# Summing two weight parts of a seven-product block form on GpSimd instead of VectorE

## The reference, cut to what matters

```
proj = rmsnorm(x, ln_g) @ w_in
q, k, v, z_a, x_b, z_b, g_a, g_b = split(proj)
...
merged = sigmoid(g_a) * (o_a @ w_a) + sigmoid(g_b) * (o_b @ w_b)
x = x + merged @ w_o
```

## Time and profile before

| | before |
|---|---|
| median of 3 runs (lowest, highest) | 1893.27 us (1892.89, 1893.54) |
| span of the profiled execution | 1889.0 us |
| time around the span, median less span | 4.3 us |
| TensorE (PE) busy | 1872.9 us, 99% |
| VectorE busy | 1306.7 us, 69% |
| ScalarE busy | 827.0 us, 44% |
| GpSimd busy | 298.6 us, 16% |

### The profile page before, as it was taken

The page is one execution under the profiler, slowest core; times in us unless marked ns, Lnnn a source line. Parts: engine busy times, 40 slices in busy tenths (PEclk is TensorE's granted clock), DMA queues, the critical chain, the costliest instruction groups (busy, mean ns, idle before and its releaser), DMA issues.

```text
span 1889.0 us, 32627 instructions
## 1 busy us (share of the span) xinstructions
PE 1872.9 (99%) x13004; PEld 1755.0 (93%) x13004; DVE 1306.7 (69%) x2260; ACT 827.0 (44%) x1352; POOL 298.6 (16%) x417
## 2 busy tenths in 40 slices
PE   9999999999999999999999999999999999999998
PEld 8899898898899999999998988988988999999997
DVE  7775665665766877866797656657557678878575
ACT  5432322423436776543444324234124377766334
POOL 2220120120231210100132201202102422001010
PEclk9999999999999999999999999999999999999999
DMA  6444534553443333543655445534444534337253
GB/s 220 137 129 159 179 132 130 163 180 110 150 147 96 104 99 99 155 134 105 199 175 162 148 124 170 178 110 152 168 119 146 167 97 107 96 93 183 90 167 116
DMA packets 119958, 264.06 MB, mean 140 GB/s; under 512 B 12510, under 2 KB 52942, under 8 KB 119678
## 3 DMA queue, kind: packets, MB, share of 16 engines
q1 hardware_dynamic: 87950, 159.94, 27.3%
q0 software_dynamic: 31712, 102.04, 17.5%
q10 hardware_dynamic: 144, 0.00, 0.0%
HBM read 203.11 MB, written 49.12 MB: 134 GB/s over the span
## 4 chain that ended last, share of the span: by engine, by line
PE 87%; DVE 5%; ACT 3%; DMA 2%; DVEq 1%; issue 1%; ACTq 1%; SPq 0%
PE bank L2414 19%; PE bank L2416 19%; PE bank L2415 19%; PE bank L2508 4%; PE bank L2509 4%; PE bank L2510 4%; PE bank L2778 2%; PE bank L2781 2%; PE bank L2780 2%; DMA w_raw<-in_w_units 2%; PE sums L2526 2%; PE sums L2508 1%; PE sums L2510 1%; PE sums L2509 1%; PE sums L2641 1%
## 5 line engine op out<-in xcount | busy, mean ns | idle before, releaser
L2414 PE MATMUL bank<-xn_hi,w_hi 128*128 128x296 f32 (+1 forms) x2016 | 603.5, 299 | 1.1 <-DVEq L2324 0.5
L2416 PE MATMUL bank<-xn_lo,w_hi 128*128 128x296 f32 (+1 forms) x2016 | 598.9, 297 | 0.0
L2415 PE MATMUL bank<-xn_hi,w_lo 128*128 128x296 f32 (+1 forms) x2016 | 598.1, 297 | 0.0
L2414 PEld LDWEIGHTS bank<-xn_hi,w_hi 128*128 128x128 f32 x2016 | 379.0, 188 | 8.4 <-issue 6.0
L671 ACT ACTIVATE w_hi<-w_raw 128x1024 fp32r<-128x1024 f32 x219 | 230.2, 1055 | 349.0 <-DMA w_raw<-in_w_units 346.4
L2415 PEld LDWEIGHTS bank<-xn_hi,w_lo 128*128 128x128 f32 x2016 | 379.5, 188 | 0.9
L2416 PEld LDWEIGHTS bank<-xn_lo,w_hi 128*128 128x128 f32 x2016 | 378.6, 188 | 0.0
L681 DVE TENSOR_TENSOR w_lo<-w_raw,w_hi 128x1024 fp32r<-128x1024 f32 x219 | 268.4, 1229 | 59.1 <-ACT w_hi L671 52.5
L2414 PE MATMUL bank<-oa_hi,w_hi 128*128 128x296 f32 (+1 forms) x512 | 153.7, 300 | 0.0
L2415 PE MATMUL bank<-oa_hi,w_lo 128*128 128x296 f32 (+1 forms) x512 | 151.9, 297 | 0.0
L2416 PE MATMUL bank<-oa_lo,w_hi 128*128 128x296 f32 (+1 forms) x512 | 151.7, 296 | 0.0
(11 more groups left out here) (347 smaller groups left out, 3846.1 us busy)
## 6 DMA issues: line engine op xcount, KB each, us to landing
w_raw<-in_w_units SPq DMA_DIRECT2D x189, 512.0 KB, 3.7
w_raw<-in_w_units SPq DMA_DIRECT2D x151, 256.0 KB, 3.4
S<-in_state_ret POOLq DMA_DIRECT2D x64, 512.0 KB, 4.8
out_ret_s<-S POOLq DMA_DIRECT2D x64, 512.0 KB, 6.2
w_raw<-in_w_units POOLq DMA_DIRECT2D x20, 256.0 KB, 4.9
vst<-v_scr SPq DMA_DIRECT2D x8, 512.0 KB, 4.1
out_ret_p<-Sp POOLq DMA_DIRECT2D x8, 512.0 KB, 5.9
v_scr<-vtok_hi SPq DMA_DIRECT2D x16, 160.0 KB
```

Source lines behind the costliest of these rows:

```text
L2414: pe.matmul(ps, w_hi[:, slot, cols], x_hi, start=first, stop=False)
L2415: pe.matmul(ps, w_lo[:, slot, cols], x_hi, start=False, stop=False)
L2416: return pe.matmul(ps, w_hi[:, slot, cols], x_lo, start=False, stop=last)
```

## The change

For the four pairs of g_b (not for the output projection's pairs) the sums S2 and S4 are made by GpSimd, between the adding transfers. GpSimd's queue per pair becomes: adding transfer of S1; wait for S2's load and for the landing of S1's transfer; add; drain; adding transfer of S3; wait for S4's load; add; drain. VectorE loses its eight adds and drains per layer and gets two waits per pair: it must not overwrite S1 before S2's sum has read it, nor S2 before S4's sum has.

```diff
@@ -960,9 +960,21 @@
+                def add_raw(two, part, other):
+
+                    n, m = two * PRODUCTS + part, two * PRODUCTS + other
+                    wait_part(pool, l, n)
+                    if other == S1:
+                        pool.wait_ge(s1_in[two % 2], 16 * pairs_like(l, two))
+                    pool.tensor_tensor(part_of(w_raw, l, n), part_of(w_raw, l, n), part_of(w_raw, l, m), ADD)\
+                        .then_inc(part_sum, 1)
+                    pool.drain()
+
                 for two in range(TILE_PAIRS):
                     add_part(two, S1)
+                    add_raw(two, S2, S1)
                     add_part(two, S3)
+                    add_raw(two, S4, S2)
                 load_early(0)
@@ -2073,6 +2085,8 @@
                     n = two * PRODUCTS + part
                     dve.wait_ge(part_hi, PART_AT[l] + n + 1)
+                    if two < TILE_PAIRS and part in (S1, S2):
+                        dve.wait_ge(part_sum, (PAIR_AT[l] + two) * 2 + (1 if part == S1 else 2))
                     dve.tensor_tensor(part_of(w_lo, l, n), part_of(w_raw, l, n), part_of(w_hi, l, n).bitcast(f32),
                                       SUB).then_inc(part_lo, 1)
@@ -2114,10 +2128,8 @@
                 part_low(0, A11)
-                part_add(0, S2, S1)
                 part_low(0, S1)
                 right_low(2, mix2_lo[:, :, 0:wide], of_right(mix2), mix2_hi[:, :, 0:wide])
-                part_add(0, S4, S2)
                 part_low(0, S2)
@@ -2138,9 +2150,7 @@
                     if more:
-                        part_add(two + 1, S2, S1)
                         part_low(two + 1, S1)
-                        part_add(two + 1, S4, S2)
                         part_low(two + 1, S2)
```

## The result

The kernel after takes 1902.15 us (median of four runs, 1900.78 to 1902.82), the kernel before 1893.08 in the same session: 1.0044 times, with a 95% interval of 1.0029 to 1.0058. That is 9.1 us slower, beyond the 0.2% (3.8 us) that a measurement can tell from no change. The profiled span is 1900.9 us, 11.9 above that of before; of this, the block forms hold 8.8, and 2.5 are one wait in layer 0's output projection, told at the end of the experiments. The spans differ by more than the medians because the profiled execution of before was a quick one: its span is 4.3 us under the median, where that of after is 1.3 under.

What follows compares the result with a forecast made beforehand. GpSimd's queue was taken to become the bound, a pair taking 14.35 us against TensorE's 11.4. Delays of 6.6 us in layer 0 and 7.0 in layer 1 made 13.6, added to 1893.3: 1906.9, range 1898.5 to 1913.

Steps and rivals of the forecast that it cites:

- VectorE's eight adds are worth nothing: Eight adds of 0.69 us per layer leave VectorE; nothing gained, since TensorE waits for a transfer, not for them.
- The add at 1.27 us: Each sum on GpSimd takes 1.27 us, as its same-size operation L887 does; upper bound 2.32.
- No contention in pairs 1 to 3: Nothing charged for GpSimd's adds and VectorE holding each other up, since VectorE then only has work waiting for the add.
- S2's drain, 2.1 from the add's start: Drain behind S2's sum, after S1's transfer landed, ends 2.1 us from the add's start, hiding the add's 1.27.
- S4's drain ends at a fixed look, 5.3: Drain behind S4's sum, with S3's transfer in flight, looks only at certain times; add and drain take 5.3 us.
- rival 1: The drain ends with the transfer's landing, not at a fixed look: 3.0 us less, 1903.9; chance 0.15.
- GpSimd's queue becomes the bound: Waits, adds, drains and issues make a pair take 14.35 us on GpSimd against 11.4 on TensorE.
- the sign against itself: S1's transfers still 12 us apart, rather than about 14, would prove the queue argument wrong.
- Lateness builds up, and pair 0 hides its drain: Pair 1's S1 is issued as before at 783.53; two pairs later S2 of pair 3 is 6.6 us late in layer 0.
- Rival 3: Drain cheap, 0.60, over with the add; S2 ready 9.5 us behind S1's issue; 1.5 us a layer, 1896.3; chance 0.07.
- What queues behind VectorE's waits adds nothing: A12's low half, gate tiles, ob_low and S3's low half need some 3.5 us against TensorE's 3.3; nothing added.
- The clock: Granted clock 1.00 in both stretches; a fall was a rival, 9.8 us more, 1916.7, chance 0.03.

Runs made afterwards that it cites:

- drains alone: Kernel before, sums still on VectorE, with GpSimd's wait for S1's landing and drains behind it and behind S3's issue added: 1893.33 us, 1.0003.
- after once more: The kernel after, unchanged, measured again beside other variants, against the kernel before: 1902.23 us, 1.0051.
- early drain: Kernel after plus one more drain in GpSimd's idle time ahead of each layer's first adding transfer: 1901.60 us, 1.0045.
- S4's sum first: Kernel after without drains, both sums back to back on GpSimd, S3's transfer issued behind them: 1906.60 us, 1.0076.

## Why the prediction was right or wrong

The sign, the range and the kind of wait were right; the size was 4.5 us too large, and the step that made it (6) had the wrong mechanism. That the range held the result is in part luck, since the sum behind it came from a queue that was not the bound.

1. **VectorE's eight adds are worth nothing.** Right: 7.9 us of VectorE gone, none of it won.
2. **The add at 1.27 us.** Right where it runs alone (1.28); up to 1.6 where it starts before the issue of a transfer is over (1.58 with 0.26 us of overlap in pair 1 of layer 0, 1.39 with 0.06 in pair 2 of layer 1). Over both layers the source line says:

```profile
L969 POOL TENSOR_TENSOR w_raw<-w_raw x16: 1281/1552/2010, 768.9 to 1754.4; 128x512 f32<-128x512 f32 x16
```

3. **No contention in pairs 1 to 3.** Right there but for 0.25 us: S2's sum in pair 1 of layer 0 took 1.53, beside a low half that had started first. It shows in pair 0, where VectorE is busy. In layer 0 the sum started first and kept its 1.28, and VectorE's 128x1184 operation beside it took 2.51 us, where those of its size before and behind it took 1.39 and 1.38. In layer 1 VectorE's operation started first and kept its 1.35, and the sum took 2.01. The Trainium skill (SBUF — State Buffer, Who interferes with whom) has this rule, and these rows agree with it, down to who holds whom.
4. **S2's drain, 2.1 from the add's start.** Wrong: 1.46 to 1.71. It ends 0.15 us behind the add, but S3's issue starts 0.64 behind the add's end, where without the drain it starts with that end: some 0.7 us in each of six pairs, 4.2. Its removal gives 3.4 us from after, and 4.7 from the kernel that has no drain behind S4's sum.
5. **S4's drain ends at a fixed look, 5.3.** Wrong in kind, near in size: 4.55 from 790.7 ends at 795.27, where ScalarE's copy of S3, released by the same landing, starts at 795.22. It ends with the landing, which was rival 1's mechanism. Rival 1's time (1903.9, measured 1902.15) is near by luck, because it too took GpSimd's queue for the bound.
6. **"GpSimd's queue becomes the bound", a pair in 14.35 us.** This is the step that failed. S1's transfers start at 783.61, 796.13 and 808.91, 12.5 and 12.8 apart (12.2 and 12.5 in layer 1), which the prediction had named as the sign against itself; each of the three waits for its part's load, not for the drain. The drains alone cost 0.4 us, and S4's drain can go without gain. The margin is small: in four of the six places the drain's end leaves some 0.4 us, in one (1733.65) none, and after once more it held S1 back by 1.5 us in pair 2 of layer 0. The prediction set the drain against the period of 11.4 us but left out that S1's part, whose load A11's end releases, can be added to only some 4.1 us behind that end (mean of before, pairs 1 to 3), so that GpSimd was idle there anyway.
7. **Lateness builds up, and pair 0 hides its drain.** Half wrong. Pair 1's S1 did start as forecast (783.61 against 783.53), but the waits come in each pair with the change, pair 0 included (1.8 us). A better sum was at hand: S2's low half came 1.62 us later behind S1's issue (9.25 less 7.63). Before, 4.13 from A11's end to S1's issue, 7.63, VectorE's 0.69 and 0.14 make 12.6 of 13.0 us, so 0.4 was spare; 1.2 paid per pair, six times, is 7.3. With pair 0's 1.8 that is 9.1, the result. The mechanism is borne out, but that the sum meets the result so exactly is luck: by TensorE's starts the six pairs lost 0.5, 0.6, 2.1, 1.9, 0.5 and 2.0 us (before lost 1.7 in all), the first leg grew from 4.1 to 4.4 us, and with the early drain pair 0's 1.8 went without a gain. How much of the 1.62 is GpSimd's longer add (1.28 to 1.58 against 0.69) and how much its place in the queue, no run separates. Rival 3 had this chain, 9.5 us without a drain's hold against 9.1, and made 3 us of it in all; without drains it measured 9.7 (8.90, 0.69 and 0.14) and cost 5.7.
8. **What queues behind VectorE's waits adds nothing.** Half right. In pair 1 of layer 0 it is just this queue (gate tiles, ob_low) that TensorE waits for at S3. The prediction had named that case and given it 1 us "inside the delay that the queue sets anyway"; without that delay it counts. So TensorE waits at S2 and at S3: of the 7.8 us in pairs 1 to 3, 3.5 and 2.8, and 1.4 at S1.
9. **The clock.** Right: 1.00 in both stretches. In two of the variants it did fall (last section).

No variant beats the kernel before; the nearest that keep a part of the change, with one sum on GpSimd or with pairs 0 and 1 alone, are 0.17% slower.

## What to carry to other kernels

Before costing a moved operation by its queue, find the loop that closes around it: which product frees the room, which load that starts, and what follows one after the other until a product needs it; a delay inside that loop can be paid in every turn, and one beside it (here a drain of 5 us) can be free. Where a low half overwrites its raw operand, every later reader of that operand stands in front of it, so such a sum belongs on the engine that writes the low half. An engine with a low busy share can still be the one that the tensor engine waits for.

## What the runs showed of the hardware

**GpSimd's drain is paid per transfer issued since the last drain.** Counting GpSimd's DMA issues in the timelines between two drains: with 1, landed, the drain takes 0.12 us; with 76 it takes 6.26 (drains alone, first of each layer, with no operation ahead of it); with 80 behind a 1.28 us add, 7.94 (with the change in pairs 2 and 3), so 6.66. That is 0.08 us each. The rows of before fit too, and were misread: 0.60 without a transfer and 2.07 with 18 differ by 1.47, 0.08 each; the fixed look at 2.1 us was that count. The 5.28 was a landing: two transfers were in flight, and the second landed 0.13 us before the drain's end. The 11.31 had 98 issues behind it (some 8 us) and a landing 7.3 us after its start; with 15 issues in place of 98 (drains alone) this drain took 7.91. How a count and a landing add up stays open. A drain in idle time clears the count, as the early drain shows. In layer 0 of the drains alone:

```profile
L966 POOLq DRAIN  x1: 6259/6259/6259, 767.4 to 767.4; - x1
```

**The granted clock fell behind some stands of TensorE, and the length of the stand alone does not say which.** With the change in pairs 2 and 3, TensorE stood for 6.8 us, and the window behind that was granted half, the lower of the two levels (1.2 GHz of 2.4), for the whole of S2's product and into A12's. With S4's sum first it stood for 2.8 us in pair 3 of layer 0 and kept 1.00. In the same execution it stood for only 1.9 us ahead of S1 in pair 1 of layer 1, and six matmuls later the grant was half: S1's and S2's products took 2.25 and 2.54 us in place of 1.59. Windows of the one, then of the other in layer 0 and in layer 1, with the columns as above, and the matmul behind the stand in layer 1:

```profile
811.00:814.50 3.50, 3.12 (x13) 3.15 (x14) 3.50 (x7) 0.63 (x1) 0.87 (x1) 0.50 0.26 28
814.50:818.00 3.50, 3.50 (x23) 3.50 (x23) 2.47 (x5) 3.22 (x7) 1.29 (x1) 0.82 0.64 139
```

```profile
825.90:829.00 3.10, 3.10 (x23) 3.10 (x24) 2.70 (x5) 3.07 (x6) 0.00 (x0) 1.00 0.14 20
1732.50:1736.00 3.50, 3.50 (x17) 3.50 (x16) 3.25 (x7) 0.61 (x2) 1.81 (x3) 0.51 0.55 85
1731.63 0.37 PE L2789 MATMUL bank<-right,w_hi 128*128 128x288 f32 x1 [1.88 <-DVE w_lo L2091]
```

The Trainium skill (TensorE: Matmul & The Clock Gate, Part 1: The HAM clock gate) says that an idle TensorE is put back to the lower level; the prediction said that no run showed it, and these two do. Which stands do it, these rows do not settle.
